# A fused two-block transformer kernel: the first block begins on half of its inner dimension, and two small computations of the mixers move

## What is computed

```python
sh1, sc1, ... = split(silu(c) @ mod_w + mod_b, 6)          # once for c, once for c_ctx
a  = rms_norm(x) * gain * (1 + sc1) + sh1                  # x:   256 x 1024
ac = rms_norm(ctx) * gain * (1 + csc1) + csh1              # ctx: 256 x 1024
q, k, v, p = split(a @ w_in, [512, 640, 768])              # 512, 128, 128, 512 columns
kc, vc = split(ac @ w_in[:, 512:768], [128])
q = rope(rms_norm(q)); k = rope(rms_norm(k)); kc = rms_norm(kc)
```

```python
# nsa, compressed path: softmax over 15 compressed keys, masked
p = exp(s - max(s)) * mask;  p = p / max(sum(p), 1e-30) * path_gate
# fox: a decay added to the scores
log_f = log_sigmoid(f + bias);  c = cumsum(log_f, axis=tokens)
s = q @ k.T / 8 + c[query] - c[key]
```

## Time and profile before

| | |
|---|---|
| median of 3 runs | 1653.5 us (1652.08 to 1653.53) |
| profiled execution | 1651.39 us |
| its span | 1649.6 us |
| mean granted TensorE clock | 0.964 |
| TensorE busy | 1542.1 us |
| VectorE, ScalarE, GpSimd busy | 808.7, 730.1, 574.1 us |
| moved by DMA | 327.22 MB, mean 198 GB/s |
| chain that ended last | TensorE 80%, VectorE 12%, ScalarE 3%, DMA 2% |

### The profile page before, as it was taken

How to read it: one execution, slowest core, us unless ns; L and a number is a source line. 1 busy time by engine, 2 the same in 40 slices (tenths; PEclk the granted TensorE clock), 3 DMA queues, 4 the chain that set the end, 5 groups by cost and what they waited for, 6 DMA issues and landing times.

```text
span 1649.6 us, 23166 instructions
## 1 busy us (share of the span) xinstructions
PE 1542.1 (93%) x9558; PEld 1240.2 (75%) x9558; DVE 808.7 (49%) x1430; ACT 730.1 (44%) x1049; POOL 574.1 (35%) x219
## 2 busy tenths in 40 slices
PE   4999989999998999989988999999999889999997
PEld 3867867875897778668667758999886667589996
DVE  2733578423867674253754462522346653635222
ACT  3434376422436664243445444444534454344442
POOL 1300025220000442223545335655535452256543
PEclk7999889999998899999989999999999899999999
DMA  9588269769734696753433354555444334445550
GB/s 385 206 318 296 83 265 342 269 230 382 292 103 186 242 337 230 253 227 104 156 127 103 140 192 162 184 185 189 159 140 133 126 103 137 177 171 196 198 180 26
DMA packets 51226, 327.22 MB, mean 198 GB/s; under 512 B 5937, under 2 KB 5937, under 8 KB 17457
## 3 DMA queue, kind: packets, MB, share of 16 engines
q1 hardware_dynamic: 51120, 325.73, 55.0%
HBM read 324.66 MB, written 1.05 MB: 197 GB/s over the span
## 4 chain that ended last, share of the span: by engine, by line
PE 80%; DVE 12%; ACT 3%; DMA 2%; issue 1%; POOL 1%; DVEq 0%; SPq 0%; ACTq 0%
PE ps L224 20%; PE ps L225 19%; PE ps L226 19%; PE ps L221 18%; DVE lo L232 4%; DMA raw<-in_wmod 2%; PE ps L2729 1%; DVE s L240 1%; POOL lo L232 1%; ACT hi L229 1%; DVE gl L232 1%; DVE rt L232 1%; DVE pb L2780 1%; PE ps L1028 1%; ACT hTh L229 0%
## 5 line engine op out<-in xcount | busy, mean ns | idle before, releaser
L232 POOL TENSOR_TENSOR lo<-raw,hi 128x2048 fp32r<-128x2048 f32 (+2 forms) x76 | 350.7, 4624 | 648.9 <-ACT hi L229 648.9
L229 ACT ACTIVATE hi<-raw 128x2048 fp32r<-128x2048 f32 (+2 forms) x192 | 350.5, 1858 | 46.7 <-POOL big L232 16.9
L232 DVE TENSOR_TENSOR lo<-raw,hi 128x2048 fp32r<-128x2048 f32 (+1 forms) x116 | 298.7, 2591 | 96.1 <-ACT hi L229 96.1
L232 POOL TENSOR_TENSOR loh<-rawh,hih 128x1024 fp32r<-128x1024 f32 x56 | 138.7, 2489 | 155.4 <-ACT hih L229 155.4
L224 PE MATMUL ps<-hTh,hi 128*128 128x256 f32 x640 | 183.2, 286 | 4.9 <-DVE hTl L232 2.9
L225 PE MATMUL ps<-hTl,hi 128*128 128x256 f32 x640 | 182.4, 285 | 0.0
L226 PE MATMUL ps<-hTh,lo 128*128 128x256 f32 x640 | 182.3, 285 | 0.0
L224 PE MATMUL ps<-hi,hTh 128*128 128x512 f32 (+3 forms) x320 | 118.3, 370 | 11.7 <-DVE hTl L232 5.6
L224 PEld LDWEIGHTS ps<-hTh,hi 128*128 128x128 f32 x640 | 124.2, 194 | 6.6 <-issue 3.5
L225 PEld LDWEIGHTS ps<-hTl,hi 128*128 128x128 f32 x640 | 124.2, 194 | 0.5
L226 PEld LDWEIGHTS ps<-hTh,lo 128*128 128x128 f32 x640 | 124.2, 194 | 0.0
(11 more groups left out here) (308 smaller groups left out, 2946.1 us busy)
## 6 DMA issues: line engine op xcount, KB each, us to landing
raw<-in_wgu SPq DMA_DIRECT2D x64, 1024.0 KB, 5.0
raw<-in_wmod SPq DMA_DIRECT2D x48, 1024.0 KB, 6.1
raw<-in_wdn SPq DMA_DIRECT2D x32, 1024.0 KB, 5.5
rawh<-in_wgt SPq DMA_DIRECT2D x64, 512.0 KB, 3.9
raw<-in_wup SPq DMA_DIRECT2D x32, 1024.0 KB, 4.8
raw<-in_wdown SPq DMA_DIRECT2D x32, 1024.0 KB, 5.1
raw<-in_wz SPq DMA_DIRECT2D x12, 1024.0 KB, 4.9
raw<-in_wbr SPq DMA_DIRECT2D x8, 1024.0 KB, 4.8
```

The source lines that it names most:

```text
L229: return self.e.activation(o, a, f, **kw)
L232: return self.e.tensor_tensor(o, a, b, op)
```

## The change

**Start.** Loads come in another order, modulation pieces 0 and 2 first, then x and ctx early with only the constants that they need (`ident`, 192 columns of `col`); the rest of the constants goes behind the weights. `t_start` makes pieces 0 and 2, the norm of inner rows 0 to 511, and the kv product over that half, then pieces 1 and 3, and the other half. kv is made with `mm` straight from its weights, without parts, and its four results share two banks. q and p are made by halves as well, and p's low parts move from GpSimd to VectorE; GpSimd has no work left there, ctx is not split at all.

**Mixers.** The logarithms of the forget gate move into the emptying of z (`a_decay`, `v_decay_in`, `v_decay`), the decay product to the front of `t_heads`, and its copy to `st`. The first padded block of fox is built one step earlier (`v_forget`). The compressed softmax leaves `v_compress` and becomes a task of the second weave (`v_shares`, `a_shares`), which begins its count at 1 on all engines.

```diff
-        return part(t_in["we_" + name], at[0], 1024 if name == "kv" else PIECE), "dve" if name == "q" else "pool"
+        return part(t_in["we_" + name], at[0], 1024 if name == "kv" else PIECE), "raw" if name == "kv" else "dve"
...
-            elif c.n == 2:
-                small("cst", self.cst[:, :], self.t_in["cst"])
-            elif c.n == 4:
-                small("col", self.col[:, :], self.t_in["colp"])
+            elif c.key == ("mod", 0, 2, 0):
+                small("ident", self.C("ident"), self.t_in["cst"][:, 0:128])
+                small("col", self.col[:, 0:NCOL1], self.t_in["colp"][:, 0:NCOL1])
                 small("x", self.x[:, :, :], self.t_in["x"])
                 small("cx", self.cx, self.t_in["ctx"])
-            elif c.n == 10:
+            elif c.key == ("p", 0):
+                small("cst", self.cst[:, 128:NCST], self.t_in["cst"][:, 128:NCST])
                 small("row", self.row[:, :], rows(0, RKEEP))
+            elif c.key == ("pm",):
+                small("col2", self.col[:, NCOL1:NCOL], self.t_in["colp"][:, NCOL1:NCOL])
...
+    def t_start(self, t):
+        x = self.x, self.s1
+        c = self.cx, self.s2
+        self.t_mod(t, 0, 0, "C")
+        self.t_mod_T(t, 0, 0, "C")
+        self.t_norm(t, "a0x", *x, "G", (0, 2))
+        self.t_mod(t, 0, 2, "C")
+        self.t_mod_T(t, 0, 2, "C")
+        self.t_norm(t, "a0c", *c, "M", (0, 2))
+        kv = [t.take("S", "kv", i) for i in range(2)]
+        self.t_keys0(t, kv, 0)
+        self.t_mod(t, 0, 1, "C")
+        self.t_norm(t, "a0x", *x, "G", (4, 6))
+        self.t_mod(t, 0, 3, "C")
+        self.t_mod_T(t, 0, 1, "C")
+        self.t_mod_T(t, 0, 3, "C")
+        q = [t.take("M", "q", i) for i in range(2)]
+        self.t_half(t, q, "q", 0, lambda: self.t_norm(t, "a0c", *c, "C", (4, 6)))
+        self.t_keys0(t, kv, 1)
+        self.t_half(t, q, "q", 1)
+        p = [t.take("G", "p", i) for i in range(2)]
+        self.t_half(t, p, "p", 0)
+        self.t_half(t, p, "p", 1)
+    def t_keys0(self, t, banks, i):
+        c = t.chunk("kv", i)
+        w = kn(c.raw, 4)
+        t.wait_ge(*t.at("landed", c.key))
+        for b, (name, f, *_) in zip(banks, self.sources0()):
+            if i == 0:
+                t.wait_ge(*t.free(b))
+            for q in range(2):
+                for k in range(4):
+                    if q == 0 and k % 2 == 0:
+                        t.wait_ge(*t.empty("norm", name, 4 * i + k))
+                    m = t.mm(self.ps[:, b, 256 * q:256 * q + 256], f[:, 4 * i + k, 128 * q:128 * q + 128], w[:, k, :],
+                             i == k == q == 0, i == q == 1 and k == 3)
+            if i:
+                m.then_inc(*t.up(f"full{b}"))
+        if i == 0:
+            m.then_inc(*t.up("pe"))
+        t.mark("used", c.key)
+    def t_half(self, t, banks, name, i, between=None):
+        c = t.chunk(name, i)
+        wh, wl = kn(c.hi, 4), kn(c.lo, 4)
+        t.wait_ge(*t.at("lo", c.key))
+        for q, b in enumerate(banks):
+            if i == 0:
+                t.wait_ge(*t.free(b))
+            for k in range(4):
+                t.wait_ge(*t.at("hT", "a0x", 2 * i + k // 2))
+                m = t.mm3(self.ps[:, b, :], [h[:, 4 * i + k, 128 * q:128 * q + 128] for h in self.H3],
+                          (wh[:, k, :], wl[:, k, :]), i == k == 0, i == 1 and k == 3)
+            if i:
+                m.then_inc(*t.up(f"full{b}"))
+            if q == 0 and between is not None:
+                between()
+        if i == 0:
+            m.then_inc(*t.up("pe"))
+        t.mark("used", c.key)
...
+    def a_half(self, a, i):
+        a.wait_ge(*a.at("scale 0", i))
+        for name, f, scale, shift in self.sources0():
+            b = a.bank("norm", name, 4 * i + 2)
+            a.wait_ge(*a.full("norm", name, 4 * i + 2))
+            for k in (4 * i + 2, 4 * i + 3):
+                j = k % 2
+                m = a.ac(f[:, k, :], self.ps[:, b, 256 * j:256 * j + 256], ACT.Identity, scale=scale[:, k:k + 1],
+                         bias=shift[:, k:k + 1])
+            m.then_inc(*a.up(f"free{b}"))
+        for k in (4 * i, 4 * i + 2):
+            a.wait_ge(*a.empty("norm", "a0x", k))
+            a.ac(self.H3[0][:, k:k + 2, :], self.hT[:, k:k + 2, :]).then_inc(*a.up("act"))
+            a.mark("hT hi", "a0x", k)
+    def v_half(self, v, i):
+        n = slice(4 * i, 4 * i + 4)
+        gain = self.K("n1a", 4 * i, 4)
+        for j in range(2):
+            v.wait_ge(*v.at("mcol", 0, j, i))
+        v.stt(self.cadj[:, 3, n], self.mcol[:, 8 + 4 * i:12 + 4 * i], 1.0, gain, ALU.add, ALU.mult)
+        v.stt(self.cadj[:, 2, n], self.cadj[:, 1, n], 1.0, gain, ALU.add, ALU.mult).then_inc(*v.up("dve"))
+        v.mark("scale 0", i)
+        v.wait_ge(*v.last)
+        for name, f, scale, shift in self.sources0():
+            b = v.bank("norm", name, 4 * i)
+            v.wait_ge(*v.full("norm", name, 4 * i))
+            for k in (4 * i, 4 * i + 1):
+                j = k % 2
+                m = v.ts(f[:, k, :], self.ps[:, b, 256 * j:256 * j + 256], scale[:, k:k + 1], shift[:, k:k + 1],
+                         ALU.mult, ALU.add)
+            m.then_inc(*v.up(f"free{b}"))
+        for k in (4 * i, 4 * i + 2):
+            v.wait_ge(*v.at("hT hi", "a0x", k))
+            v.tt(self.H3[1][:, k:k + 2, :], self.hT[:, k:k + 2, :], self.H3[0][:, k:k + 2, :].bitcast(F32),
+                 ALU.subtract).then_inc(*v.up("dve"))
+            v.mark("hT", "a0x", k // 2)
...
+            if i == 3:
+                self.a_decay(a, l)
...
+            if i == 2:
+                self.v_decay_in(v, l)
+            elif i == 4:
+                self.v_decay(v, l)
...
+        self.t_decay(t, l)
...
+        self.v_decay_out(v, l)
...
+    def a_shares(self, a, l):
+        V, ps = self.views2(), self.ps
         p3 = V.pcp.rearrange("p t h c -> p (t h) c")
         a.wait_ge(*a.at("cmp less", l))
         a.ac(p3, p3, ACT.Exp, scale=0.125).then_inc(*a.up("act"))
         a.mark("cmp exp", l)
-        yield
...
+    def v_shares(self, v, l):
+        V = self.views2()
+        cm = self.C("cmul")
+        p3 = V.pcp.rearrange("p t h c -> p (t h) c")
+        m_, sm = self.st[:, 100:108], self.st[:, 108:116]
+        mu = [bc(cm[:, 15 * t:15 * t + 15], 4) for t in range(2)]
         v.wait_ge(*v.last)
         v.red(m_, p3, ALU.max).then_inc(*v.up("dve"))
         v.wait_ge(*v.last)
...
         v.mark("cmp prob", l)
-        yield
+        for _ in range(self.SHARES_AFTER):
+            yield
...
+    def v_decay_in(self, v, l):
+        f, g_ = self.logs()
+        v.wait_ge(*v.empty("z", l, 0, 0))
+        v.wait_ge(*v.empty("z", l, 0, 1))
         v.tt(f, self.z[:, :, SM + 12:SM + 16], bc(self.R("fb", 4 * l, 4), 2), ALU.add).then_inc(*v.up("dve"))
         v.wait_ge(*v.last)
         v.stt(g_, f, -1.0, f, ALU.mult, ALU.min).then_inc(*v.up("dve"))
         v.mark("f low", l)
+
+    def v_decay(self, v, l):
+        f, g_ = self.logs()
         v.wait_ge(*v.at("f log", l))
         v.stt(f, f, 0.0, g_, ALU.min, ALU.subtract).then_inc(*v.up("dve"))
         v.mark("log f", l)
...
+            if t == 0:
+                yield
...
-               self.v_latent(v, l), self.v_top(v, l), (None for _ in range(self.SHARES_AFTER))], 5,
-              paced(step, *PACE[1]))
+               self.v_latent(v, l), self.v_top(v, l), self.v_shares(v, l)], 5,
+              paced(step, *PACE[1], 1))
...
+        self.a_mod(a, 0, 0)
         self.a_stats(a, "a0x", self.x, lambda h, t: a.at("in", "x"), self.s1, 0, ("sil",))
         self.a_stats(a, "a0c", self.cx, lambda h, t: a.at("in", "cx"), self.s2, 32)
-        for p in range(4):
-            self.a_mod(a, 0, p)
-        self.a_split(a, "kv", 0, ahead=1)
-        self.a_norm(a, "a0x", self.cadj[:, 3, :], self.mcol[:, 0:8], self.hT, H, [("scale", 0, 0)], [])
-        self.a_norm(a, "a0c", self.cadj[:, 2, :], self.cadj[:, 0, :], self.hTc(), Y, [("scale c",)], [])
-        self.a_split(a, "kv", 1)
-        self.a_split(a, "q", 1)
+        self.a_mod(a, 0, 2)
+        self.a_half(a, 0)
+        self.a_split(a, "q", 0, ahead=0)
+        self.a_mod(a, 0, 1)
+        self.a_mod(a, 0, 3)
+        self.a_split(a, "q", 1, ahead=0)
+        self.a_half(a, 1)
+        self.a_split(a, "p", 1, ahead=0)
...
+        mod = lambda p: self.v_mod(v, 0, p, self.cadj[:, p // 2, 4 * (p % 2):4 * (p % 2) + 4])
         self.v_diag(v, "a0x", self.s1, 0)
         self.v_diag(v, "a0c", self.s2, 32)
-        for p in range(4):
-            self.v_mod(v, 0, p, self.cadj[:, p // 2, 4 * (p % 2):4 * (p % 2) + 4])
-        v.wait_ge(*v.last)
-        v.stt(self.cadj[:, 2, :], self.cadj[:, 1, :], 1.0, self.K("n1a", 0, 8), ALU.add,
-              ALU.mult).then_inc(*v.up("dve"))
-        v.mark("scale c")
-        self.v_cond_scale(v, 0, 0, self.K("n1a", 0, 8))
-        self.v_norm(v, "a0x", self.cadj[:, 3, :], self.mcol[:, 0:8], self.hT, H, [("scale", 0, 0)], [])
```

(14 more changed lines are left out.)

99 lines of the change are left out of this document (47 added, 52 removed).

## The result

| | before | after |
|---|---|---|
| time, median of four executions | 1653.5 us (1652.1 to 1655.3) | 1638.8 us (1636.7 to 1642.3) |
| ratio, 95% interval | | 0.9909 (0.989 to 0.9928) |
| profiled execution | 1651.4 us, span 1649.6 | 1642.3 us, span 1640.6 |
| TensorE busy | 1542.1 us | 1548.2 us |

A second set of five runs of the same kernel gave 1640.0 us, ratio 0.9918 (0.9902 to 0.9933). The change gains 14 to 15 us where the forecast had 35. Faster was right, the size was not, and the time lies above the range (1610 to 1637). The profiled execution of the kernel after is the longest of its four, 3.5 us above the median.

What follows compares the result with a forecast made beforehand. TensorE, busy 1542.1 of 1649.6 us, bounds the kernel; only its idle time and clock can give. Start 7 + softmax 2 x 7.5 + logarithms 2 x 6.5 = 35 us, so 1618.5 us, range 1610 to 1637.

Steps and rivals of the forecast that it cites:

- The start: New load order and split inner dimension before the heads: p done at 70.9 us instead of 77.95, 7 us gained.
- rival (d): Slower: the 1.2 GHz level of 20 to 25 us lasts through the new, sparser start; 1655 us, chance 0.02.
- The cover on VectorE: VectorE's chain from kv to the query factors ends at 70.3 us, wanted at 77.9; 77.4 if GpSimd's 7.1 us stay.
- The logarithms: Forget logarithms leave the mixers' tanh: stall, low clock and padded-block wait go, 6.5 us a layer (4 to 7.3).
- the 2.6 us less: By the page, the moved table load holds the index work about 1.3 us in each layer, 2.6 us less gain.
- The compressed softmax: Softmax moved and pacing started earlier in the mixers: stalls and low clock around the first scores go, 7.5 us a layer.
- The probabilities have about 15 us of TensorE work as cover: Softmax ahead of the probabilities stays covered in the mixers; if the cover fails it costs 1 to 3 us.
- rival (b): Mixers give half: late exponential or late probabilities make new stalls that bring the low clock; 1632.5 us, chance 0.13.
- Such a stall brings no low clock: At the forget logarithms' tanh, the remaining 0.65 us stall leaves full clock: 12 products by 0.2, 2.4 us.
- TensorE waits 1.23 us and 4.64 us around the first two scores for VectorE's maxima: Both mixer waits counted as removed, 1.23 + 4.64 us of the 8.6 us a layer before deductions.

Runs made afterwards that it cites:

- mixed fills: Changed kernel with gate fills behind odd steps up to the ninth and even ones from the twelfth, so both score pairs have one between them: 1631.5 us.
- early fills alone: Changed kernel with only the compressed softmax put back at its old place, the pacing still starting one step earlier: 1632.0 us.

## Why the prediction was wrong, step by step

**The start: right.** 7 us forecast, 7.24 measured at the heads and 7.1 to 11.4 by the run alone, p done at 70.2 us against 70.9, kv begun at 26.18 against 25.5. The granted clock is 1.00 from 10 to 70 us in the profile after, so rival (d) is out. The cover on VectorE was larger than needed: even with GpSimd at work the heads begin only 0.23 us later.

**The logarithms: right.** 6.5 us a layer forecast; 7.3 in layer 0 and 7.6 in layer 1 by the matched traces, less the 0.65 that the decay products cost at their new place (forecast 0.7), so 6.6 and 7.0; 14.7 for both in the run alone. TensorE waits 0.75 us for the tanh, forecast 0.65. The moved table load takes 1.28 us from 793.88 us on, the tanh starts at 795.17, and ScalarE still idles 0.37 us ahead of the index work as before, so the 2.6 us less that the prediction named beside its sum did not come.

**The compressed softmax: wrong,** 15 us forecast, 4 us lost by the medians (1639.4, the mean of both, less 1635.3) and 9 on the stretch itself by the traces. The sum treated the wait of 4.64 us as removed by two edits together, which it was; the failure lies in what it left beside. Five steps failed.

- "The probabilities have about 15 us of TensorE work as cover (five fills and small products), against some 13 us of VectorE work with one slow step in it." There were four slow steps, not one: softmax 10.6 us instead of 4.7. I knew of the 2.21 us step and named it in rival (b), yet did not look at what ended it. GpSimd's row in the trace of before was there to find. It runs from 824.13 to 826.47, and the step of 2.21 us ends at 826.49:

```profile
824.13 2.34 POOL L232 TENSOR_TENSOR loh<-rawh,hih 128x1024 fp32r<-128x1024 f32 x1 [2.98 <-ACT hih L229]
```

- The earlier pacing was followed only to the first pair of scores. It shifts every later fill too, and at the scores of i=1 it took one away that covered VectorE's maxima. That term was never priced; it measures 2.4 us of wait a layer (1.87 to 4.30), and 8 us in the whole kernel with its low clock (changed against mixed fills).
- "Such a stall brings no low clock (1.23 before the first scores did not)." At the tanh it held, but I took it for the softmax's small remaining stalls too. In the kernel after, waits of 0.98 and 0.78 us were followed by a window at 0.66. One row is not a rule, and this row did not even show it: in the trace of before the granted clock is 0.50 from 825.8 us on, 0.2 us into the stall of 4.64 us and 0.9 us after the wait of 1.23 us had ended, so it can't be said which of the two brought it.
- The two edits were summed as if each had its own wait to remove. They share one: each takes 2.9 us of it, and only the last 2.0 us need both.
- "TensorE waits 1.23 us and 4.64 us around the first two scores for VectorE's maxima", and the sum takes both away. The wait of 1.23 us is ended by ScalarE. With the early fills alone it stands unchanged (1.26 and 1.24 us), with the moved softmax it is 0.78 with a new 0.98 ahead of it. This term of 1.2 us a layer had no edit behind it.

Rival (b) had the mechanism, "late probabilities" and "new stalls that are long enough to bring the low clock again", at 0.13 and at half the gain. It should have reached to no gain at all from the softmax: 7 + 13 = 20, or 1633.5. The measured start and logarithms together gave 1635.3.

The Trainium skill (SBUF — State Buffer, section "Who interferes with whom") has the rule that the prediction needed: a VectorE instruction with two SBUF inputs and a GpSimd instruction that reads SBUF exclude each other, and the one that comes second waits for the whole of the other. The traces agree: the stretched products end with a low part, and they shrink from 2.89 to 1.46 us when the low parts are halved. One step with a single input stretched as well, the one of 8 elements (L237): 1.96 us where it took 0.17 in the kernel before. With that rule the nine steps could have been laid against the low parts in the window of the old trace.

## What to carry to other kernels

When work is moved on an engine, lay each of its small steps against what the neighbour engine runs there, and price it at the rest of that neighbour's instruction, not at its own duration. When a pacing is shifted, follow it to its end and write down which pair of steps loses the filler it had; two cures of one wait are one term of the sum. Where the parts of a change may lean on each other, measure the corners: here neither edit alone lost, and both together did. With the fills mixed, the softmax one step later and the low parts in halves, 35.6 us were there, the size of the forecast, but by two more edits than it had priced.

## What the runs showed of the hardware

**A small VectorE step costs what is left of GpSimd's instruction.** 0.17 to 0.3 us of work took up to 2.4 us against instructions of 2.37 us, and 0.85 to 1.3 against halves of about 1.25. Not every form suffers: between the same low parts the reductions and the steps that pick the top values kept their 0.28 and 0.43 us.

**The same wait brings the low clock in one execution and not in another.** Both kernels wait 0.79 us for VectorE before the same product. First the kernel before, then the one after:

```profile
162.05 0.50 PE L224 MATMUL ps<-hi,yTh 128*128 128x512 f32 x1 [0.79 <-DVE lo L232]
...
163.10 0.40 PE L225 MATMUL ps<-lo,yTh 128*128 128x512 f32 x1
```

```profile
154.81 0.50 PE L225 MATMUL ps<-hi,yTh 128*128 128x512 f32 x1 [0.79 <-DVE lo L233]
...
156.10 0.63 PE L226 MATMUL ps<-lo,yTh 128*128 128x512 f32 x1
```

The rows' durations overlap; from start to start a product takes 0.23 us there at the full clock and 0.42 at the lower one, and the kernel after loses 1.56 us there of its lead of 7.24. In the second profile of the same kernel the window of 155 to 160 us is at 1.00. The executions of one kernel lie 1 to 12 us apart here, so a term of 2 us has to be read from the waits, not from two medians.
